# Moving the first product pieces two modulation chunks sooner, and the first operand tiles ahead of half a weight split

## The reference

```python
c_act = jax.nn.silu(c)
mod = c_act @ w_ada[l] + b_ada[l]
shift, scale, gate = jnp.split(mod, 3, axis=-1)
h = _layernorm(x) * (1.0 + scale[:, None, :]) + shift[:, None, :]
p = h @ w_in[l]
```

## Time and profile before

| | us |
| --- | --- |
| median of 3 runs | 2121.85 (2115.71 to 2122.82) |
| the profiled execution | 2120.68 |
| its span, first to last instruction | 2118.9 |
| TensorE busy | 2031.8 (96%) |
| mean granted clock of TensorE | 0.989 |

### The profile page before, as it was taken

How to read it: one execution, slowest core, us unless ns; L and a number is a source line. 1 busy time by engine, 2 the same in 40 slices (tenths; PEclk the granted TensorE clock), 3 DMA queues, 4 the chain that set the end, 5 groups by cost and what they waited for, 6 DMA issues and landing times.

```text
span 2118.9 us, 36630 instructions
## 1 busy us (share of the span) xinstructions
PE 2031.8 (96%) x14264; PEld 1845.7 (87%) x14264; DVE 1378.4 (65%) x1891; ACT 935.2 (44%) x1390; POOL 29.7 (1%) x59
## 2 busy tenths in 40 slices
PE   5999999998999999799999999999999999999998
PEld 2789888768999988799999999889889989989986
DVE  5457677686588867888998545565545545545555
ACT  3344445444545553433336334454434434433443
POOL 0000000000000000000000000000000000000000
PEclk8999999998999999999999999999999999999999
DMA  9988877874557665245454555534555555555553
GB/s 381 397 323 303 314 301 293 304 275 176 199 201 276 231 225 201 102 177 181 176 179 164 214 181 195 215 143 178 199 187 190 182 195 185 191 193 183 185 193 138
DMA packets 64403, 462.40 MB, mean 218 GB/s; under 512 B 7264, under 2 KB 7808, under 8 KB 8368
## 3 DMA queue, kind: packets, MB, share of 16 engines
q1 hardware_dynamic: 57152, 410.49, 52.7%
q0 software_dynamic: 7152, 50.51, 6.4%
HBM read 458.85 MB, written 2.13 MB: 218 GB/s over the span
## 4 chain that ended last, share of the span: by engine, by line
PE 66%; DVE 8%; ACT 2%; issue 1%; DVEq 0%; ACTq 0%
PE ps L523 22%; PE ps L524 22%; PE ps L525 22%; DVE w_lo L1694 3%; DVE area L1730 1%; ACT w_hi L1148 1%; DVE st L1714 1%; PE ps L565 1%; ACT sc L1400 0%; ACT sc L1406 0%; DVE X L2162 0%; DVE grow L2259 0%; DVE csil L2109 0%; DVE area L2259 0%; DVE y_lo L1714 0%
## 5 line engine op out<-in xcount | busy, mean ns | idle before, releaser
L1694 DVE TENSOR_TENSOR w_lo<-raw,w_hi 128x1024 fp32r<-128x1024 f32 x642 | 758.4, 1221 | 389.8 <-ACT w_hi L1148 386.7
L1148 ACT CAST w_hi<-raw 128x1024 fp32r<-128x1024 f32 (+1 forms) x642 | 640.8, 1047 | 457.2 <-PE ps L525 444.5
L523 PE MATMUL ps<-a_hi,w_lo 128*128 128x256 f32 (+1 forms) x2912 | 828.1, 284 | 14.8 <-DVE w_lo L1694 8.2
L524 PE MATMUL ps<-a_lo,w_hi 128*128 128x256 f32 (+1 forms) x2912 | 824.0, 283 | 0.0
L525 PE MATMUL ps<-a_hi,w_hi 128*128 128x256 f32 (+1 forms) x2912 | 823.0, 283 | 0.0
L523 PEld LDWEIGHTS ps<-a_hi,w_lo 128*128 128x128 f32 x2912 | 552.0, 190 | 43.7 <-issue 33.1
L525 PEld LDWEIGHTS ps<-a_hi,w_hi 128*128 128x128 f32 x2912 | 552.2, 190 | 0.0
L524 PEld LDWEIGHTS ps<-a_lo,w_hi 128*128 128x128 f32 x2912 | 549.5, 189 | 0.7 <-issue 0.5
L523 PE MATMUL ps<-w_hi,y_lo 128*128 128x512 f32 x720 | 282.1, 392 | 4.2 <-DVE w_lo L1694 2.5
L525 PE MATMUL ps<-w_hi,y_hi 128*128 128x512 f32 x720 | 281.0, 390 | 0.0
L524 PE MATMUL ps<-w_lo,y_hi 128*128 128x512 f32 x720 | 280.9, 390 | 0.0
(11 more groups left out here) (274 smaller groups left out, 2030.6 us busy)
## 6 DMA issues: line engine op xcount, KB each, us to landing
raw<-in_stream SPq DMA_DIRECT2D x331, 1024.0 KB, 4.8
area<-in_ada SPq DMA_DIRECT2D x46, 1024.0 KB, 7.5
area<-in_ada POOLq DMA_DIRECT2D x40, 1024.0 KB, 5.7
grow<-in_ada SPq DMA_DIRECT2D x10, 1024.0 KB, 5.4
area<-in_rows POOLq DMA_DIRECT2D x4, 1024.0 KB, 5.4
X<-in_x SPq DMA_DIRECT2D x1, 2048.0 KB, 9.1
grow<-row_scratch POOLq DMA_DIRECT2D x2, 1024.0 KB, 6.0
grow<-in_rows POOLq DMA_DIRECT2D x2, 1024.0 KB, 5.1
```

The costliest lines, as they stand in the source:

```text
L523: pe.matmul(o, w[1], a[0], start=first, stop=False, skip_group_check=shared)
L524: pe.matmul(o, w[0], a[1], start=False, stop=False, skip_group_check=shared)
L1148: ac.copy(to, raw[:, bass.ds((g % RAW) * CH + h * n, n)]).then_inc(hi_ready, 1)
L1694: ve.tensor_tensor(to, raw[:, bass.ds((g % RAW) * CH + h * n, n)], hi.bitcast(F32), ALU.subtract).then_inc(lo_ready, 1)
```

## The change

TensorE places pieces by another rule. Before, the pieces with p < (c - 9) * 3 // 2 stood behind chunk c; now it is p < min((c - 8) * 3 // 2 + 1, 12 * ((c - 1) // 8)). The two waits that protect the banks move from chunk 9 to chunk 7. The last `turn_row` moves from ahead of piece 34 to behind piece 35. On DVE, for the first quarter only, `read_mod0(0)` goes ahead of the subtraction of weight chunk 0, whose first half follows it, and whose second half stands between the two `split_modulated`. On ACT the second half of weight chunk 0 is rounded behind `modulated(0, 0)`.

Number of pieces placed by the end of chunk c:

| c | 9 | 10 | 11 | 12 | 13 | 14 | 15 | 16 | 17 | 18 | 19 | 30 | 31 |
| --- | --- | --- | --- | --- | --- | --- | --- | --- | --- | --- | --- | --- | --- |
| before | 0 | 1 | 3 | 4 | 6 | 7 | 9 | 10 | 12 | 13 | 15 | 31 | 33 |
| after | 2 | 4 | 5 | 7 | 8 | 10 | 11 | 12 | 14 | 16 | 17 | 34 | 35 |

```diff
                 ada_chunk(c)
                 if 2 <= c < 6:
                     turn_tokens(0, c - 2)
-                if c == 9:
+                if c == 7:
                     pe.wait_ge(ln_var, NORM["meta"] + 1)
                     pe.wait_ge(xn_l, 4)
-                while p < (c - 9) * 3 // 2:
+                while c >= 8 and p < min((c - 8) * 3 // 2 + 1, 12 * ((c - 1) // 8)):
                     piece(0, p // 12, p % 12 // 4, p % 4)
                     p += 1
             while p < 36:
                 piece(0, p // 12, p % 12 // 4, p % 4)
                 p += 1
-                if p == 34:
+                if p == 36:
                     turn_row(ADA0 // 4 - 1)
             last_quarter(0)
...
             for q in range(3):
-                split(3 * q, q % 2, q % 2)
+                split(3 * q, q % 2, q % 2, halves=range(1 if q == 0 else 2))
                 ac.wait_ge(col_in, q + 1)
                 modulated(0, q)
+                if q == 0:
+                    split(0, 0, 0, halves=(1,))
                 take_row(2 * q + 2)
...
             for q in range(4):
-                split(3 * q, q % 2)
+                if q:
+                    split(3 * q, q % 2)
                 read_mod0(q)
+                if q == 0:
+                    split(0, 0, halves=(0,))
                 split_modulated(0, 2 * q)
+                if q == 0:
+                    split(0, 0, halves=(1,))
                 split_modulated(0, 2 * q + 1)
```

## The result

The changed kernel is slower: 2140.97 us (median of 4 runs, 2137.38 to 2145.58) against 2122.34 before (also four runs by now), a ratio of 1.0089 with a 95% interval of 1.0072 to 1.0106, that is 15 to 22 us. The profiled execution took 2138.11 us, its span is 2136.4.

The account below looks back on a forecast made before the run. TensorE was taken as the bound from chunk 10 on, the transfers ahead of it. 11.2 us of waits net of the front plus 3.2 us of clock gave +14.4 us, so 2136 us, range 2127 to 2143.

Parts of the forecast that it names:

- The front: Ahead of chunk 10: pieces 0 and 1 behind chunk 9 fill 3.17 us of TensorE idle time, a gain.
- The weight waits: Pieces 4, 16, 28 behind chunks 11, 19, 27 wait for weight chunks ACT rounds late: three times 2.9, 8.7 us lost.
- The quarter waits: Pieces 12 and 24 behind chunks 17 and 25 wait for their quarter's first pair: 1.6 us twice, 3.2 us lost.
- The end: At the last quarter, the final turned row loses its cover of two pieces: about 3.6 us wait for 0.69, 2.9 more.
- The sum at full clock: Shift of the last quarter's start: -3.2 + 8.7 + 3.2 + 2.9 = 11.6, or 11.2 us after swallowing chunk 19's 0.45.
- The clock: Behind the longer TensorE waits, about two of four bring half clock: 3.2 us lost, bounds 0 to 6.8.
- The rival of the clock: The clock falls at nearly every wait, some stretches doubled: 21 to 23 us lost, 2143 to 2145 us; chance 0.12.
- The third rival: Weight waits real but mostly repaid by earlier clock rise and shorter quarter waits, no fall: 2126 to 2129 us; chance 0.13.
- The rival of the DMA as the true bound: TensorE's new waits fall into time it would have stood for landings: 2119 to 2122 us, not slower; chance 0.09.

Follow-up runs that it names:

- the first two experiments: Changed kernel with ACT and DVE as before: 2142.57 us; changed kernel with TensorE's order as before, other edits kept: 2121.00 us.
- the front alone: Kernel before with only pieces 0 and 1 behind chunk 9 and the two bank waits behind chunk 7: 2119.98 us, ratio 0.9990.
- the tail as before: Changed kernel with no piece beyond 31 ahead of chunk 31 and the last turned row ahead of piece 34 again: 2134.88 us, ratio 1.0053.
- the order alone: Changed kernel with the edits on ACT and DVE taken back, only TensorE's new order kept: 2142.57 us, ratio 1.0090.
- the halves' order: Changed kernel with quarter 0's order of ACT and DVE used for quarters 1 and 2 too: 2137.57 us, ratio 1.0084.

## Why the prediction was right

**The front.** Foretold: 3.2 us of idle time filled, piece 0 free to start behind chunk 9 even without the edits of ACT and DVE. The profile shows it, and the first two experiments show that the edits are worth nothing within the intervals (0.9982 to 1.0015 for the edits alone). What was not foreseen is that a part of the 3.2 us comes back as landings once TensorE runs ahead (2.35 us of them in the front alone, and 1.1 us less idle time in all). In the changed kernel this didn't matter, since its waits let the transfers get ahead.

**The weight waits.** Foretold 2.9 us three times, measured 2.91 three times. The mechanism (ACT rounds behind the row that the chunk itself releases) is shown from both sides, by moving the pieces and by moving the rounding: either takes the three waits away.

**The quarter waits.** Foretold 1.6 us twice, measured 1.56 twice. They vanish when DVE reads the modulation ahead of its subtraction, and puts one half of it in front of the pair in place of two.

**The end.** Foretold some 3.6 us in place of 0.69, measured 3.68. With the tail as before it is 0.69 again.

**The sum at full clock.** Foretold 11.2 us, measured 11.45 us more idle time in the stretch. That the rest of the program only shifts held as far as one can tell: behind the last quarter's start it took 2.75 us more, within the 6.6 us by which this part differs among the fourteen profiles. It gave nothing back.

**The clock.** This is the term that was mis-sized, at both of its ends. I took 3.2 us: about two falls at 1.7, and nothing for an earlier rise. The number of falls in the changed kernel's profile was two, at piece 16 and at the last quarter. But a low stretch was 6.8 us long both times, and 6.8, 10.2, 3.4 and 6.8 us in the order alone, where the row that I priced from had 3.4 us; so one fall costs up to 3.4 or 5 us, half of its length, when TensorE is busy throughout. Against that stands the earlier rise, which I had bounded at 2.3 us and put at nothing because pieces 0 and 1 are slow themselves; it gave back 2.7 us in the profile. It belongs to the order: full clock comes 1.1 to 6.2 us behind the start of chunk 9 in the eleven profiles with pieces 0 and 1 behind that chunk, and 9.0 to 10.6 us in the three without.

The size of the whole term comes by subtraction. Of the runs' 18.9 us (0.0089 of 2122), 11.5 are idle time, and some 7 are left, 4 to 11 by the interval. The same subtraction (the change of the time by the ratio, less the change of the idle time in the stretch) leaves 8 and 9 us for the order alone and the halves' order, which have the three weight waits and the long one at the end too, 3 us with the tail as before, and -2.4 to 2.0 us for the nine kernels without all three weight waits. Each is uncertain by 2 to 5 us. So the clock's cost seems to go with the weight waits and the last one. The mean granted clock of the four runs was 0.980 to 0.987 (mean 0.983), where that of the kernel before was 0.984 to 0.991 in the executions measured beside the experiments (mean 0.987). With 7 in place of 3.2 us the forecast of 2136 would have been 2140. Its two errors, falls priced too short and no earlier rise, partly cancelled. The rival of the clock, with more falls and doubled ones, was the nearer in its price though not in its count: no wait of 1.56 us was followed by a fall. The third rival was right that the clock rises sooner, and wrong that the weight waits are mostly repaid.

The rival of the DMA as the true bound fell for this change (0.8 us of landings left in the stretch) and holds for orders that put TensorE further ahead, as two experiments show.

## What to carry to other kernels

When work is placed sooner in one engine's queue, read in the other engines' queues what its operand is queued behind: a piece put directly behind the chunk whose use releases the copy ahead of its rounding waits for that whole chain, however early the data have landed. An idle time at the front of a stretch that two resources nearly fill together can be worth less than its length, since the other one takes over as soon as it is filled (here 3.2 us filled, 2.35 of landings back). And work kept as cover for the last dependent chain must not be spent earlier, because the sum of work stays and only the cover moves.

## What the runs showed of the hardware

The same six waits, to 0.1 us, gave a stretch of 102.4 us in one kernel and 109.0 us in another that differ only in edits worth nothing. The difference is the granted clock: low for 6.8 us (88.4 to 95.2) within the one up to 143 us, and for 6.8, 10.2 and 3.4 us in the other (from 55.9, 90.0 and 127.4 us), besides 2.7 us more at the front. A wait of 2.91 us ahead of 55.53 us was followed by no fall in the changed kernel, and the same wait ahead of 55.40 us in the order alone was followed by one from 55.9 us on. So a wait of this length brings a cost that varies by several us from one profile to the next, and a single profile can hide or invent 3 us.

Over all fourteen profiles, from behind chunk 10 to 153 us, the waits of TensorE sort by length. None of 1.86 us or less was followed by half clock. The three of 1.95, 2.03 and 2.27 us all were. Of thirteen waits of 2.91 us nine were and four were not, and of the six of 3.45 to 3.74 us all were. (For some of them the clock fell before the wait had ended.) What lets four of the thirteen pass isn't settled by these runs.

Landing waits of 0.45 to 2.3 us turned up at chunks 13, 18, 19, 24, 26 or 29 in orders that should not have differed there (0.45 at chunk 19 in the earlier trace rows, 2.03 at chunk 18 in one run and 2.27 in another). Their cause stays open.
